# RWKV inverse, levels 1 to 4: transposes of 128x128 instead of a third set of 64x64 products, and no crossed layout

## What is computed

```python
def rwkv7_scan(r, w, k, v, kk, a, reverse):
    B, S, H, N = r.shape

    def step(state, inp):
        r_t, w_t, k_t, v_t, kk_t, a_t = inp
        sa = jnp.einsum('bhij,bhj->bhi', state, -kk_t)
        state = (state * w_t[:, :, None, :]
                 + sa[..., None] * (kk_t * a_t)[:, :, None, :]
                 + v_t[..., None] * k_t[:, :, None, :])
        y_t = jnp.einsum('bhij,bhj->bhi', state, r_t)
        return state, y_t
...
    y = (rwkv7_scan(r_h, decay[:, :, 0], k_dir[:, :, 0], v_h, kk, a[:, :, 0], False)
         + rwkv7_scan(r_h, decay[:, :, 1], k_dir[:, :, 1], v_h, kk, a[:, :, 1], True))
```

## Time and profile before

| | |
|---|---|
| time, median of 3 runs (lowest, highest) | 2341.51 us (2339.97, 2343.05) |
| span of the profiled execution | 2341.0 us |
| TensorE busy | 2245.5 us, 96% |
| VectorE, ScalarE, GpSimd busy | 1193.9, 947.8, 898.2 us |
| the RWKV stage's first and last TensorE product | at 1358.9 and 1586.5 us |
| granted TensorE clock | full in nearly all of the 40 slices |

### The profile page before, as it was taken

One profiled execution on the slowest core, in us unless ns is written; L12 is line 12 of the kernel. 1 busy time (PEld: TensorE's weight loads), 2 busy tenths in 40 slices (PEclk: granted clock), 3 DMA queues, 4 the chain that ended last, 5 costly groups with the idle time before them and its releaser, 6 DMA issues. The chain is left out here.

```text
span 2341.0 us, 38427 instructions
## 1 busy us (share of the span) xinstructions
PE 2245.5 (96%) x16046; PEld 1743.2 (74%) x16046; DVE 1193.9 (51%) x2014; ACT 947.8 (40%) x1364; POOL 898.2 (38%) x678
## 2 busy tenths in 40 slices
PE   7999999999999999999999988878999999999997
PEld 5776777787877857777788777776666778888885
DVE  5544834334245467342343878854644657317334
ACT  5423355345353324654343433324266342222243
POOL 4342343334434404333344422222333445545543
PEclk9999999999999999999999989999999999999998
DMA  4221221222222202222233200002211232232332
GB/s 159 84 85 36 73 90 64 72 73 85 98 81 81 90 22 87 81 66 79 68 106 104 72 3 4 4 19 77 72 64 57 81 105 91 99 99 91 99 99 72
DMA packets 50568, 175.18 MB, mean 75 GB/s; under 512 B 6036, under 2 KB 7004, under 8 KB 50396
## 3 DMA queue, kind: packets, MB, share of 16 engines
q1 hardware_dynamic: 50396, 172.73, 22.5%
HBM read 170.60 MB, written 2.11 MB: 74 GB/s over the span
## 5 line engine op out<-in xcount | busy, mean ns | idle before, releaser
L349 POOL TENSOR_TENSOR w_low<-work,w_high 128x512 fp32r<-128x512 f32 x622 | 835.6, 1365 | 1245.2 <-ACT w_high L298 1245.2
L279 PE MATMUL ps<-x_high_tiles,w_high 128*128 128x512 f32 x1544 | 624.9, 405 | 17.5 <-POOL w_low L349 10.9
L298 ACT ACTIVATE w_high<-work 128x1024 fp32r<-128x1024 f32 x311 | 329.2, 1059 | 733.7 <-PE ps L279 730.3
L279 PE MATMUL ps<-x_low_tiles,w_high 128*128 128x512 f32 x1544 | 604.0, 391 | 0.8 <-DVE x_low_tiles L371 0.8
L279 PE MATMUL ps<-x_high_tiles,w_low 128*128 128x512 f32 x1544 | 603.5, 391 | 0.0
L279 PE MATMUL ps<-arena_parts,w_high 128*128 128x512 f32 x1264 | 397.6, 391 | 4.3 <-DVE arena L437 1.6
L279 PEld LDWEIGHTS ps<-x_high_tiles,w_high 128*128 128x128 f32 x1544 | 291.0, 188 | 118.4 <-issue 44.5
L279 PEld LDWEIGHTS ps<-x_low_tiles,w_high 128*128 128x128 f32 x1544 | 290.9, 188 | 64.2 <-DVE x_low_tiles L371 1.6
L279 PEld LDWEIGHTS ps<-x_high_tiles,w_low 128*128 128x128 f32 x1544 | 291.4, 189 | 63.3 <-issue 6.0
L279 PEld LDWEIGHTS ps<-arena_parts,w_high 128*128 128x128 f32 x1264 | 237.3, 188 | 56.8 <-issue 3.2
L279 PE MATMUL ps<-arena_parts,w_low 128*128 128x512 f32 x608 | 236.6, 389 | 0.0
(11 more groups left out here) (452 smaller groups left out, 2864.5 us busy)
## 6 DMA issues: line engine op xcount, KB each, us to landing
work<-w_first SPq DMA_DIRECT2D x178, 512.0 KB, 3.7
work<-w_second SPq DMA_DIRECT2D x134, 512.0 KB, 3.6
xT_sb<-xT SPq DMA_DIRECT2D x8, 256.0 KB, 6.0
outT<-arena SPq DMA_DIRECT2D x8, 256.0 KB, 2.1
arena<-distance_bias SPq DMA_DIRECT2D x4, 256.0 KB
small<-small SPq DMA_DIRECT2D x1, 815.5 KB, 4.5
arena<-consts SPq DMA_DIRECT2D x1, 544.0 KB, 3.8
base<-consts SPq DMA_DIRECT2D x1, 512.0 KB
```

Of the source, the lines that this page charges most:

```text
L279: ins = pe.matmul(out, lhsT, rhs, start=(n == 0 and k == 0 and q == 0), stop=(n == unit["granules"] - 1 and k == len(ops[i]) - 1 and q == 2))
L298: act.activation(m.wh[:, split_of(g), :], m.raw[:, raw_of(g), :], ACT.Copy).then_inc(sem["high_ready"], 1)
L349: pool.tensor_tensor(m.wl[:, split_of(g), part], m.raw[:, raw_of(g), part], m.wh[:, split_of(g), part].bitcast(F32), ALU.subtract).then_in ...
```

## The change

- The crossed layout goes. `kap` and `rho` are written with their chunks in another order (`paired`), so that each product finds its operands in an order in which four quadrants can be used. `straight`, and the split of `within` into smaller matmuls in odd chunks, go.
- In levels 1 to 4 `MT` is no longer made by `transposed` and a VectorE subtraction. At the start of every level, 1 to 5, TensorE transposes `M` (`turned_inverse`, four 128x128 transposes for each way) and ScalarE copies the result to `MT`. `transposed` and its subtraction stay in level 5 alone.
- VectorE no longer makes the first `MT` (three instructions for each way).
- `BV` and PZ use four quadrants instead of two.

```diff
@@ rwkv_stage, tensor
+            def by_level(w):
+
+                for j in range(T):
+                    for p, h in QUADS:
+                        cols = slice(64 * (2 * j + h), 64 * (2 * j + h) + 64)
+                        ins = pe.matmul(m.ps[HALF[h], w.bank + p, 64 * j:64 * j + 64], w.L[HALF[p], cols], w.M[HALF[p], cols],
                                         start=True, stop=True)
                 return ins
...
+            def turned_inverse(w):
+
+                for j in range(T):
+                    ins = pe.transpose(bank(w, 3)[:, j * P:(j + 1) * P], w.M[:, j * P:(j + 1) * P], m.ident)
                 return ins
...
-                    straight(w, (0, 1), w.bet_of(i), w.kap_of(i))
                     within(w, (0, 1), w.kap_of(i), w.bet_of(i), 1).then_inc(sem[f"a_ready{w.d}"], 1)
...
                     for w in ways:
                         pe.wait_ge(sem[f"lev_ready{w.d}"], LAST * i + n)
                         pe.wait_ge(sem[f"m_ready{w.d}"], LAST * i + n)
-                        product(w, w.L, w.M, crossed_in=1).then_inc(sem[f"t1_ready{w.d}"], 1)
+                        by_level(w).then_inc(sem[f"t1_ready{w.d}"], 1)
+                    for w in ways:
+                        if n == 1:
+                            pe.wait_ge(sem[f"bv_copied{w.d}"], i + 1)
+                        turned_inverse(w).then_inc(sem[f"xt_ready{w.d}"], 1)
                     beside(i, 2 * n - 2)
                     for w in ways:
                         pe.wait_ge(sem[f"t1_copied{w.d}"], LAST * i + n)
                         pe.wait_ge(sem[f"mt_ready{w.d}"], (LAST + 1) * i + n)
                         if n < LAST:
-                            product(w, w.MT, w.T1, crossed_out=1).then_inc(sem[f"x_ready{w.d}"], 1)
-                    for w in ways:
-                        transposed(w).then_inc(sem[f"xt_ready{w.d}"], 1)
+                            by_inverse(w).then_inc(sem[f"x_ready{w.d}"], 1)
+                        else:
+                            transposed(w).then_inc(sem[f"xt_ready{w.d}"], 1)
                     beside(i, 2 * n - 1)
@@ rwkv_stage, scalar
                         act.activation(by_turns(w.T1), two_banks(m, w), ACT.Copy).then_inc(sem[f"t1_copied{w.d}"], 1)
+                    for w in ways:
+                        act.wait_ge(sem[f"xt_ready{w.d}"], (LAST + 1) * i + n)
+                        act.activation(w.MT, m.ps[:, w.bank + 3, :], ACT.Copy).then_inc(sem[f"mt_ready{w.d}"], 1)
                     beside(i, 2 * n - 2)
@@ rwkv_stage, vector
                 for w in ways:
-                    some = every(w.lev[:, 0:64])[:, 0:4, :]
-                    own.op(dve.tensor_tensor(ch(w.MT)[:, 0:NCH:2, :], ch(w.AT)[:, 0:NCH:2, :], some, ALU.mult))
                     a = m.ps[:, w.bank:w.bank + 2, :].rearrange("p a (t x n) -> p (a t) x n", x=2, n=64)
                     dve.wait_ge(sem[f"a_ready{w.d}"], i + 1)
                     own.op(dve.tensor_tensor(ch(w.M), a[:, :, 0, :], every(w.levT[:, 0:64]), ALU.mult))
-                    own.op(dve.tensor_tensor(ch(w.MT)[:, 1:NCH:2, :], a[:, 1:NCH:2, 1, :], some, ALU.mult))
...
-                    dve.tensor_tensor(ch(w.MT), eye, ch(w.MT), ALU.subtract).then_inc(sem[f"mt_ready{w.d}"], 1)
...
-                    for w in ways:
-                        dve.wait_ge(sem[f"xt_ready{w.d}"], LAST * i + n)
-                        dve.wait_ge(sem[f"mt_ready{w.d}"], (LAST + 1) * i + n)
-                        dve.tensor_tensor(w.MT, w.MT, m.ps[:, w.bank + 3, :], ALU.subtract).then_inc(sem[f"mt_ready{w.d}"], 1)
+                        else:
+                            dve.wait_ge(sem[f"xt_ready{w.d}"], (LAST + 1) * (i + 1))
+                            dve.wait_ge(sem[f"mt_ready{w.d}"], (LAST + 1) * i + n)
+                            dve.tensor_tensor(w.MT, w.MT, m.ps[:, w.bank + 3, :], ALU.subtract).then_inc(sem[f"mt_ready{w.d}"], 1)
```

More of the change, by code:

```diff
@@ L1644, in vector @@
             dve.wait_ge(sem["first_exp_ready"], 3 * d + 3)
-            own.op(dve.tensor_tensor(kap, kk[:, 0, :], ex, ALU.mult))
+            own.op(dve.tensor_tensor(paired(kap), plain(kk[:, 0, :]), plain(ex), ALU.mult))
             own.op(dve.tensor_tensor(bet, a, ex_neg, ALU.mult))
-            own.op(dve.tensor_tensor(rho, m.rw_u[:, 0, :], ex_in, ALU.mult))
+            own.op(dve.tensor_tensor(paired(rho), plain(m.rw_u[:, 0, :]), plain(ex_in), ALU.mult))
             own.op(dve.tensor_tensor(kha, kds[d], ex_neg, ALU.mult))
@@ L1829, in within @@
                         c = 2 * t + p
[L1830 to L1835, removed]
+                        cs, at = slice(c * 64, c * 64 + 64), turn_of(t) * P
@@ L1850, in straight, with by_inverse @@
                                         start=True, stop=True)
                 return ins
[L1853 to L1859, removed]
+            def by_inverse(w):
+                for j in range(T):
+                    for h, p in QUADS:
+                        cols = slice(64 * (2 * j + p), 64 * (2 * j + p) + 64)
+                        ins = pe.matmul(m.ps[HALF[p], w.bank + h, 64 * j:64 * j + 64], w.MT[HALF[h], cols], w.T1[HALF[h], cols],
+                                        start=True, stop=True)
+                return ins
@@ L1865, in transposed @@
                     cols = slice(64 * x, 64 * x + 64)
-                    for p in range(2):
-                        ins = pe.matmul(bank(w, 3)[HALF[p], cols], w.T1[HALF[p], cols], w.MT[HALF[p], cols], start=True, stop=True)
+                    for h in range(2):
+                        ins = pe.matmul(bank(w, 3)[HALF[h], cols], w.T1[HALF[h], cols], w.MT[HALF[h], cols], start=True, stop=True)
                 return ins
@@ L1914, in walk_out @@
                             ins = pe.matmul(m.ps[HALF[hh], 6, c * 64:c * 64 + 64], w.state(m, n)[HALF[hh], :],
-                                            w.rho[i % 2][HALF[hh], c * 64:c * 64 + 64], start=(n == 1 and w.d == 0),
+                                            w.rho[i % 2][HALF[hh], pair_place(c):pair_place(c) + 64], start=(n == 1 and w.d == 0),
                                             stop=(n == NCH - 1 and w.d == 1))
@@ L1952, in _ @@
                     pe.wait_ge(sem[f"mk_masked{w.d}"], i + 1)
[L1953 to L1957 removed]
+                    for j in range(T):
+                        for p, h in QUADS:
+                            x, t = 2 * j + h, 2 * h + j % 2
+                            cols, v = slice(64 * x, 64 * x + 64), i * P + 64 * (j // 2)
+                            ins = pe.matmul(m.ps[HALF[h], w.bank + 2 + p, 64 * j:64 * j + 64], w.BT[HALF[p], cols],
+                                            m.rw_vtok[HALF[p], t, v:v + 64], start=True, stop=True)
                     ins.then_inc(sem[f"bv_ready{w.d}"], 1)
@@ L1976, in _ @@
                     pe.wait_ge(sem[f"tok_ready{w.d}"], 3 * i + 1)
-                    for x in range(NCH):
-                        for p in range(2):
-                            ins = pe.matmul(m.ps[HALF[p], w.bank + x // T, (x % T) * P:(x % T) * P + P],
-                                            w.MT[HALF[p], 64 * x:64 * x + 64], w.cat[HALF[p], x, :], start=True, stop=True)
+                    for j in range(T):
+                        for h, p in QUADS:
+                            x = 2 * j + p
+                            ins = pe.matmul(m.ps[HALF[p], w.bank + h, j * P:j * P + P],
+                                            w.MT[HALF[h], 64 * x:64 * x + 64], w.cat[HALF[h], x, :], start=True, stop=True)
                     ins.then_inc(sem[f"pz_ready{w.d}"], 1)
```

61 lines of the change are left out of this document (33 added, 28 removed).

## The result

The changed kernel takes 2325.3 us, median of 4 runs (2324.93 to 2330.45), beside 2340.86 us of the kernel before, measured with it (2339.97 to 2343.05): a ratio of 0.9937, 95% interval 0.9923 to 0.9951. That is 15.6 us faster by the medians and 14.7 by the ratio. The forecast was 2327.5 us. The profiled execution has a span of 2323.7 us, 17.3 less than before.

What follows compares the result with a forecast made beforehand. TensorE's instructions, arriving in blocks of 256 records every 3.8 to 4 us, were taken to pace the stretches, with engine waits in levels; gains of 17.0 us less 3 for late blocks took 2341.5 to 2327.5 us, range 2314 to 2338.

Steps and rivals of the forecast that it cites:

- three signs that it gave for itself being wrong: Wrong if level 4 does not grow, stretches between levels shrink over 3 us each, or the clock falls within levels.
- last ending: End of the stage's last pass: 1.0 us gained, as PZ is shorter and nothing else is.
- first opening: Start of the stage: four half-width masks gone from in front of T1, 1.3 us gained.
- levels of pass 1: Pass 1: levels 1 and 2 give 1.7 us, levels 4 and 5 take 1.6 back, 0.1 gained.
- levels of pass 2, of pass 3: Per pass, levels 1 to 3 gain 1.2, 1.0, 0.15; levels 4 and 5 lose 1.0, 0.55: 0.8 us gained.
- levels of pass 4: Pass 4, without `lora`, exponentials or `sums`: levels take 25.6 us for 32.5, 7.0 gained.
- three stretches between levels: Pass endings with next openings: half a block of 3.9 us less in each, 2.0 us each, 6.0 in all.
- late blocks in the levels, all passes: Instruction blocks arriving late in the shortened levels cost 3 us, from 0 to 13, over some 27 blocks.
- its bound of 3.4 us each: Upper bound per stretch from shorter durations: BV 1.1, PZ 1.8, `straight` 0.5 us.
- The rival by which the stalls have nothing to do with records: Stretches gain 3.4 us each, nothing is set off in the levels: 2320.3 us, chance 0.05.
- the 1.0 us forecast: Passes 1 to 3: two ScalarE copies ahead of the table load make level 4 longer by 1.0 us.
- 1.00 in all levels: TensorE's granted clock stays at 1.00 through the levels; the rival with a falling clock, 2351 us, had chance 0.10.

Runs made afterwards that it cites:

- first experiment: Changed kernel with each 128-column matmul of `within` split into two of 64, 256 records more per pass: 2339.03 us, ratio to the kernel before 0.9988.
- last experiment: Kernel before, with ScalarE's turned copies ahead of the exponentials in levels 4 and 5: 2339.52 us, ratio to the kernel before 0.9996.
- third experiment: Changed kernel with ScalarE's turned copies ahead of the exponentials in levels 4 and 5, second way's exponentials in slot 8: 2317.75 us, ratio to the kernel before 0.9892.
- sixth experiment: Changed kernel with all three SyncE weight loads waiting for the last products of the last pass: 2330.16 us, ratio to the kernel before 0.9956.

## Why the prediction came out right, and where its terms were off

The time was met within 2.2 us, and the mechanisms that it names are in the trace: instruction blocks pace the stretches, VectorE comes last in level 3 (TensorE waits 1.2 us there in passes 2 and 3), ScalarE in level 4, and level 2 takes 5.76 us for 5.6. But two of the three signs that it gave for itself being wrong came true: the stretches shrank by more than 3 us in two cases of three, and the clock fell within the levels. That the sum is so near is in part luck. On the stage the forecast is 3.7 us too small: the opening, pass 1 and the stretches gave 5.4 us more than forecast and the 3 us for late blocks were not needed, while passes 2 and 4 and the last ending gave 4.8 less.

| term, gain in us | predicted | measured |
|---|---|---|
| first opening | 1.3 | 2.0 |
| levels of pass 1 | 0.1 | 1.2 |
| levels of pass 2, of pass 3 | 0.8, 0.8 | -1.1, 0.9 |
| levels of pass 4 | 7.0 | 5.2 |
| three stretches between levels | 6.0 | 9.6 |
| last ending | 1.0 | -0.1 |
| late blocks in the levels, all passes | -3 | none added; within the levels' rows |
| sum | 14.0 | 17.7 (span: 17.3) |

**The stretches** were the largest error, 3.2 us each for 2.0. The prediction took half a block less, at 3.9 us a block. The mechanism held: a block more costs 3.4 to 4.05 us, with hardly any TensorE work in it (first experiment). What was mis-sized is the step from records to time: a stretch took 3.9 us for 256 records before (23.55 us for 1538) and 3.6 after (19.9 for 1411). The first experiment has more records in a stretch than the kernel before (1667), and took 23.4 to 24.05 us for them, again 3.6 to 3.7 for 256. So the new layout did more than take out half a block. The shorter BV and PZ may be it, which the prediction had as its bound of 3.4 us each; no run changes them alone. The spacing of two stalls does not settle it, as it was 3.46 and 3.50 us in the first stretch of the first experiment and 4.02 and 3.79 in the second. The rival by which the stalls have nothing to do with records came near in size (3.4 each), but the first experiment rules it out. With it falls, for this stage, the rule of the Trainium skill that the prediction named there ("Runtime: NRT & Kernel Launch", "Instruction fetch mechanics"), that crossing into the next block is mostly hidden. That rival's own 2320.3 us would have been 5 us too low.

**Late blocks in the levels** were set at 3 us against the gain. They cost less than before: TensorE's idle time of no shown cause within the four sets of levels was 6.7 us before and is 2.3 after. The levels also hold fewer blocks than the prediction's 27, by the windows 24.6.

**Levels at full clock** were right term by term. In pass 3: level 1 6.28 us (predicted 6.4), level 2 5.76 (5.6), level 3 6.35 (6.25), level 4 8.71 (9.0), level 5 5.2 (5.8). Level 4 grew by the 1.0 us forecast (7.73 to 8.71), but not quite for the reason given: the prediction took ScalarE to be last there before, with nothing of TensorE behind to hide it. The last experiment shows that TensorE was as late itself. The removal of `transposed` uncovered ScalarE's chain, and the two copies lengthened it. In pass 3, at equal clock, the third experiment took 2.8 us of level 4 back, more than the two copies are long (1.05).

**Pass 1** gave 1.2 us for 0.1. Its level 1 gave 2.6 us, in part because `transposed` ran there partly at the lower clock before (3.05 us, 2.03 in the earlier trace rows), and levels 4 and 5 took 2.4 back.

**Pass 4** gave 5.2 instead of 7.0. Its levels 1 to 3 are 4.3, 4.7 and 5.2 us for 4.4 to 4.6, level 5 is 5.2 for 5.8, and level 4 takes 7.9 for 6.0, with two stalls of 0.64 and 0.83 us, most of what late blocks still cost in the levels.

**The clock.** The forecast counted on 1.00 in all levels; apart from the start of pass 1's levels, where it was low before too, it was low from the wait for ScalarE in level 4 into level 5, in two passes of three. In pass 2 that wait is 2.67 us, as the prediction had described it, and the clock is 0.79 over level 4. In pass 1 it is 1.79 us, and the clock is 0.97 over level 4 and 0.77 over level 5. Pass 2's levels are 2.75 us longer than pass 3's, which have the same work at full clock; the miss there, 1.1 us lost for 0.8 gained, is less than that. The wait alone does not decide it: pass 3 has one of 2.68 us and kept its clock, while pass 2 of the third experiment has none in level 4 and shows 0.90 over its levels, from a fall at their beginning. What sets the moment of a fall stays open. The Trainium skill's "TensorE: Matmul & The Clock Gate", "Part 4: PE-mode transpose", says that the full clock does not engage for transposes, as they do not count as busy in the same way. No run shows the transposes as a cause: in the third experiment there are as many, and level 4 is at full clock in every pass. No run takes them out at an equal wait either, so that they have no part in it is not shown.

**The last ending** kept its length, though its products did not. From the first of PZ to the stage's last they take 12.9 us for 14.4 before, with the two late blocks at 4.5 us in all for 4.7 before. The gain was lost behind them, in a path that the prediction had at nothing: the stage ends only when SyncE's three weight loads have landed. Issue of the third load, SyncE's wait, VectorE's last instruction and the first product behind the stage, in the changed kernel:

```profile
1566.62 0.33 SPq L1837 DMA_DIRECT2D work<-w_second  x1
SPq L1839 <- DMA work<-w_second: 3.8, 1, 3.8
1568.63 0.68 DVE L2251 TENSOR_TENSOR arena<-ps,arena 128x512 f32<-128x512 f32 x1
1572.06 0.69 PE L2274 MATMUL ps<-arena 64*64 64x64 f32 x8 [4.08 <-PEq L91]
```

SyncE's wait and that product, in the kernel before:

```profile
SPq L1814 <- DMA work<-w_second: 3.3, 1, 3.3
1589.22 0.45 PE L2242 MATMUL ps<-arena 64*64 64x64 f32 x8 [2.47 <-PEq L91]
```

Before, the third load was issued at 1583.50 us and had landed at about 1587.1, ahead of VectorE's last instruction (to 1588.1 us). After, it lands at about 1570.7, 1.4 us behind VectorE's last (1569.3), and the next stage starts 1.3 us later. In the sixth experiment the loads land at about 1573.8 us, and the next stage starts 1.4 us later as well.

## What to carry to other kernels

When a set of TensorE products is removed, look for what it was hiding: here it was a ScalarE copy behind a table load and exponentials, and moving that copy, worth nothing before, gave half as much again as the change. Where TensorE works in many small tiles, as here, count instruction records before columns. The version with the copies first is the one to keep (2317.75 us); taking out the next wait gave nothing that can be told, and in the pass that was read late blocks took its place. A stage that also loads for the next one may end with its loads and not with its work: here the last load hid what the shorter PZ gave.

## What was not expected of the hardware

- TensorE's instruction blocks of 256 records come late when large loads run: 2.6 and 1.9 us of stall beside three loads of 512 KB, 1.2 and 1.4 without them, in one profiled execution of each.
- One VectorE operation on 128x512, `L2149`, took 1.75 us in level 4 of pass 2 of the third experiment and 0.68 in level 5 of its pass 3. The long ones stand beside GpSimd's masks in the rows seen; that these are the cause was not tried.
- The clock fell behind one wait of 2.7 us (pass 2) and of 1.8 us (pass 1), while each stretch between levels, with 5.2 us or more of 20 idle, kept it at 1.00. In the third experiment it was low at the start of pass 2's levels, right behind such a stretch.
